# A decoder step on one core: the long output projections as a 2x2 block product in seven multiplications

## What is computed

```python
def conv_ffn(h, prev, w_in, conv_w, conv_b, w_out):
    a, v = jnp.split(h @ w_in, 2, axis=-1)              # 1024 -> 2 x 2816, "up"
    a, buf = causal_dwconv(a, prev, conv_w)             # 3 taps over the tokens
    return (jax.nn.silu(a + conv_b) * v) @ w_out, buf   # g (1032 x 2816) @ (2816 x 1024), "down"
...
    h = rmsnorm(x, norm_ffn_pre) * (1 + sc2) + sh2
    o, buf = conv_ffn(h, ...)
    x = x + g2 * rmsnorm(o, norm_ffn_post)
```

## Time and profile before

| | |
|---|---|
| median of 3 runs | 2589.6 us (2580.55 to 2592.13) |
| profiled execution: its own time, its span | 2581.3 us, 2579.5 us |
| TensorE busy, weight loads | 2450.6 us (95%), 2323.9 us (90%) |
| VectorE, ScalarE, GpSimd busy | 1628.6 us (63%), 947.8 us (37%), 139.7 us (5%) |
| mean granted TensorE clock | 0.981 |
| memory read, written | 289.2 MB, 51.8 MB |

### The profile page before, as it was taken

The page is one execution under the profiler, slowest core; times in us unless marked ns, Lnnn a source line. Parts: engine busy times, 40 slices in busy tenths (PEclk is TensorE's granted clock), DMA queues, the critical chain, the costliest instruction groups (busy, mean ns, idle before and its releaser), DMA issues. The chain is left out here.

```text
span 2579.5 us, 44995 instructions
## 1 busy us (share of the span) xinstructions
PE 2450.6 (95%) x19182; PEld 2323.9 (90%) x19182; DVE 1628.6 (63%) x2523; ACT 947.8 (37%) x1636; POOL 139.7 (5%) x213
## 2 busy tenths in 40 slices
PE   7999999989999999999999998789989999999997
PEld 5888999989999989999975887569989999989996
DVE  6422247887777765665455666967887777764553
ACT  4211124533333334543334664024533333334432
POOL 1000000000000010000002000210000000010000
PEclk8999999999999999999999999899999999999998
DMA  9677232222222265655010033872222222265653
GB/s 351 224 259 271 87 97 97 94 82 75 75 75 88 72 209 181 189 171 181 17 33 21 21 145 129 333 272 78 83 91 75 75 75 78 83 202 181 180 174 109
DMA packets 325191, 343.70 MB, mean 133 GB/s; under 512 B 14701, under 2 KB 297106, under 8 KB 312381
## 3 DMA queue, kind: packets, MB, share of 16 engines
q1 hardware_dynamic: 301393, 205.48, 26.0%
q0 software_dynamic: 23600, 135.35, 13.8%
HBM read 289.19 MB, written 51.82 MB: 132 GB/s over the span
## 5 line engine op out<-in xcount | busy, mean ns | idle before, releaser
L1587 DVE TENSOR_TENSOR w_lo<-w_raw,w_hi 128x1024 fp32r<-128x1024 f32 (+1 forms) x198 | 227.0, 1158 | 199.3 <-ACT w_hi L1056 195.3
L1056 ACT ACTIVATE w_hi<-w_raw 128x1024 fp32r<-128x1024 f32 (+1 forms) x198 | 197.2, 1006 | 303.6 <-DMA w_raw<-in_ffn_w_out 146.5
L2505 PE MATMUL ps<-h_hi,w_hi 128*128 128x344 f32 x816 | 265.5, 325 | 4.6 <-DVE latn L2153 3.8
L2507 PE MATMUL ps<-h_hi,w_lo 128*128 128x344 f32 x816 | 261.9, 321 | 0.0
L2506 PE MATMUL ps<-h_lo,w_hi 128*128 128x344 f32 x816 | 261.9, 321 | 0.0
L2565 PE MATMUL ps<-h_hi,w_hi 128*128 128x344 f32 x608 | 196.5, 323 | 3.4 <-DVE w_lo L1587 1.7
L2567 PE MATMUL ps<-h_hi,w_lo 128*128 128x344 f32 x608 | 194.2, 319 | 0.0
L2566 PE MATMUL ps<-h_lo,w_hi 128*128 128x344 f32 x608 | 194.0, 319 | 0.0
L1324 ACT ACTIVATE op_hi_Y<-op_raw_Y 128x512 fp32r<-128x512 f32 x80 | 50.5, 632 | 327.0 <-DVE op_raw_Y L2021 164.8
L2505 PEld LDWEIGHTS ps<-h_hi,w_hi 128*128 128x128 f32 x816 | 154.8, 190 | 9.3 <-issue 8.3
L2507 PEld LDWEIGHTS ps<-h_hi,w_lo 128*128 128x128 f32 x816 | 154.6, 189 | 0.0
(11 more groups left out here) (422 smaller groups left out, 6353.6 us busy)
## 6 DMA issues: line engine op xcount, KB each, us to landing
w_raw<-in_ffn_w_out SPq DMA_DIRECT2D x96, 512.0 KB, 4.1
...
w_raw<-in_ffn_w_out SPq DMA_DIRECT2D x48, 384.0 KB, 3.4
xc<-x_d POOLq DMA_DIRECT2D x12, 1376.0 KB, 7.2
x_d<-xc POOLq DMA_DIRECT2D x9, 1376.0 KB, 5.8
...
```

Source lines behind the costliest of these rows:

```text
L1056: act.activation(w_hi[k.slot][:, 0:k.kt, :], w_raw[k.slot][:, 0:k.kt, :], ACT.Copy).then_inc(hi_ready, 1)
L1587: dve.tensor_tensor(w_lo[k.slot][:, 0:k.kt, :], w_raw[k.slot][:, 0:k.kt, :], w_hi[k.slot][:, 0:k.kt, :].bitcast(F32), ALU.subtract).then_i ...
L2505: pe.matmul(o, w_hi[k.slot][:, t, :], h_hi[:, t, up_cols(c)], start=t == 0, stop=False)
L2507: ins = pe.matmul(o, w_lo[k.slot][:, t, :], h_hi[:, t, up_cols(c)], start=False, stop=t == KD - 1)
```

## The change

Two thirds of the tokens (c = 0 and 1) are now computed as a product of 2x2 blocks: the 22 K-tiles are two halves of 11, the 8 output tiles two halves of 4, and the thirds are the two token blocks. Seven products P1 to P7 of 4 tiles each replace eight. A product tile is 33 matmuls in two weight blocks of 6 and 5 K-tiles (`PARTS11`). The last third is computed as before, in blocks of 6, 6, 6 and 4. All blocks of the stage go through five slots of 6 K-tiles, so there are 56 + 32 = 88 blocks instead of 72.

- Four products (P6, P7, P5, P4) need sums of weight blocks. GpSimd's queue makes them in memory (`wsum_d`) during the up stage, by copying transfers and transfers that add to their destination (`weight_sums`), 44 per layer, one part after each of 16 stores of g; each part waits for the part before.
- Four products (P6, P7, P5, P3) need sums of activation blocks. VectorE makes them (`stage_sum`, four sums of 11x344 columns) in the place where h stood (`hh`), after GpSimd has loaded the blocks there; each operand then passes ScalarE and VectorE as pieces of 3 to 8 K-tiles (`piece_hi`, `piece_lo`, `HI_AT`, `LO_AT`).
- Results are put together from P1's copy and the banks (`combine`); products P2, P7, P3 and P4 add on in banks that an earlier product left.
- Two of the three thirds are finished after the product tiles: the scaling of third 0 stands in product tile 26, that of third 1 among the tiles of the last third, as `xk`, `od_sb` and `ss_d`.
- The tail transposes stand after the first product tile, in banks 3, 4, 6 and 7.

```diff
--- before.py
+++ after.py
-PARTS22 = [(0, 8), (8, 16), (16, 22)]
+PARTS22 = [(0, 6), (6, 12), (12, 18), (18, 22)]
+KW = KF // 2
+PARTS11 = [(0, 6), (6, KW)]
...
+WOPS = ["P1", "P2", "P6", "P7", "P5", "P3", "P4"]
+PIECES = {"P1": (0, 1), "P2": (2, None), "P6": (3, 4), "P7": (5, 6), "P5": (7, 8), "P3": (9, 10), "P4": (11, 12)}
+NPC = 17
+NW = len(WOPS) * KH * len(PARTS11)
...
+            loads[RAW_SEM[s]] += 16 * (dmas[n] if dmas else 1)
+            held = max([last[s]] + [last[u] for u in SHARED.get(s, ())])
...
-    after = [[4, 2, 3, 0, 1][n % 5] for n in range(NU * KD * len(PARTS22))]
-    down_kt = [k1 - k0 for k0, k1 in PARTS22] * (KD * NU)
+    down_kt = [k1 - k0 for k0, k1 in PARTS11] * (len(WOPS) * KH) + [k1 - k0 for k0, k1 in PARTS22] * KD
+    after = [9 + n % 5 for n in range(len(down_kt))]
...
+    d_at = [A_W + n * D6 for n in (6, 4, 8, 0, 2)]
...
+                            if t == 2 * KH:
+                                sp.wait_ge(wsum_in, 16 * 44 * (l + 1))
...
+            def weight_sums(l, f):
+
+                q, part = f // 4, f % 4
+                rows = slice(q * ROWS, (q + 1) * ROWS)
+                low = slice(KW * P + q * ROWS, KW * P + (q + 1) * ROWS)
+                c1, c2 = slice(0, KH * P), slice(KH * P, KD * P)
+                w, v = ffn_w_out[l], wsum_d[l]
+                if part:
+                    pool.wait_ge(wsum_in, 16 * (44 * l + 11 * q + (4, 8, 10)[part - 1]))
+                if part == 0:
+                    pool.dma_start(v[0][rows, :], w[rows, c1]).then_inc(wsum_in, 16)
...
+                elif part == 1:
+                    pool.dma_start(v[0][rows, :], w[rows, c2], accum_op=ALU.add).then_inc(wsum_in, 16)
...
+                elif part == 2:
+                    pool.dma_start(v[1][rows, :], w[low, c2], accum_op=ALU.add).then_inc(wsum_in, 16)
...
+                    pool.dma_start(v[3][rows, :], w[low, c1], accum_op=ALU.add).then_inc(wsum_in, 16)
...
+            LO_AT = {5: (3,), 6: (4,), 9: (5,), 10: (6,), 13: (7,), 14: (8,), 17: (9,), 18: (10,), 21: (11,), 22: (12,),
+                     23: (13,), 25: (14,), 26: (15,)}
+            SUM_AT = {2: (0,), 3: (1,), 4: (2,), 11: (3,)}
+            ADD_AT = {5 + s: s for s in range(KH)}
+            ADD_AT.update({13 + s: s for s in range(KH, 15)})
...
+                    if stage != "sc" and 2 <= f < 18:
+                        weight_sums(int(stage == "f1"), f - 2)
...
+            def wino_moves(d):
+
+                ready = AL0[DOWN[d]]
+                pool.wait_ge(al_ready, ready + 7)
+                load_stage(1, stage_r[0], act_d[1, :, KW:KF, :])
+                pool.wait_ge(al_ready, ready + 9)
+                load_stage(2, stage_r[1][:, 0:3, :], act_d[2, :, KF - 3:KF, :])
+                pool.wait_ge(al_ready, ready + 11)
+                load_stage(0, h_raw[:, :, up_cols(2)], act_d[2, :, KW:KW + KD, :])
+                pool.wait_ge(w_done, wino_block(d, 6 * KH - 1, 1).done)
+                load_piece(d, 14, act_d[2, :, 0:7, :])
+                load_piece(d, 15, act_d[2, :, 7:KW, :])
+                pool.wait_ge(w_done, wino_block(d, 7 * KH - 1, 1).done)
+                load_x(d, 1)
...
+                for t in range(len(WOPS) * KH):
+                    i0, op, j = b + 2 * t, WOPS[t // KH], t % KH
+                    hi_to(i0 + 4)
+                    if op == "P1":
+                        copy_one(d, j)
+                    if op == "P2":
+                        copy_two(d, j)
+                    hi_to(i0 + 5)
+                    if op in ("P5", "P3", "P4"):
+                        square_tile(d, KH * (("P5", "P3", "P4").index(op) + 1) + j)
+                    for i in HI_AT.get(t, ()):
+                        piece_hi(d, i)
+                    if t == 25:
+                        root(q_post(d, 0))
...
+                out, x, y, op = ((a22, a21, a22, ALU.subtract), (a21, a11, a21, ALU.subtract), (a11, a22, a11, ALU.subtract),
+                                 (a12, a12, a11, ALU.add))[n]
...
+            def combine(d, t):
+
+                op, j = WOPS[t // KH], t % KH
+                l = d // 2
+                one, up = od_sb[:, j, :], KH + j
+                o = bank((BANKS_B if op in ("P6", "P7", "P4") else BANKS_A)[j])[:, 0:UC]
+                dve.wait_ge(w_done, wino_block(d, t, 1).done)
+                if op in ("P6", "P7"):
+                    dve.wait_ge(one_copied, KH * l + j + 1)
+                    out, x, y, f = (o_sb if op == "P6" else od_sb)[:, up, :], one, o, ALU.add
+                elif op == "P4":
+                    out, x, y, f = one, one, o, ALU.add
+                else:
+                    out = (od_sb if op == "P5" else o_sb)[:, up, :]
+                    dve.wait_ge(comb_done, 20 * l + (KH if op == "P5" else 0) + j + 1)
+                    x, y, f = o, out, ALU.subtract
+                dve.tensor_tensor(out, x, y, f).then_inc(comb_done, 1)
...
+                for t in range(len(WOPS) * KH):
+                    i0, op = b + 2 * t, WOPS[t // KH]
+                    lo_to(i0 + 4)
+                    if op not in ("P1", "P2"):
+                        combine(d, t)
+                    if t in ADD_AT:
+                        add_wino(d, ADD_AT[t])
+                    lo_to(i0 + 5)
+                    if t == 0:
+                        tails_out(KF, t0)
+                    for n in SUM_AT.get(t, ()):
+                        stage_sum(d, n)
+                    for i in LO_AT.get(t, ()):
+                        piece_lo(d, i)
+                    if t == 25:
+                        inv_root(q_post(d, 0))
+                    if t == 26:
+                        rs_in(q_post(d, 0))
+                        scale_tiles(d, 0, G, range(KD))
...
+                    if more and m == 2:
+                        rs_in(q_post(d, 1))
+                        scale_tiles(d, 1, G, range(KD))
...
+                if op == "P2":
+                    pe.wait_ge(one_copied, KH * l + j + 1)
+                if op == "P6" and j == 0:
+                    pe.wait_ge(tail_e, 2 + 6 * (l + 1))
+                if op in ("P7", "P3", "P4"):
+                    pe.wait_ge(comb_done, 20 * l + {"P7": 0, "P4": KH, "P3": 2 * KH}[op] + j + 1)
+                if op == "P5":
+                    pe.wait_ge(o_e, 24 * d + j + 1)
...
+                        hi, lo = operand(o, k)
+                        pe.matmul(out, w_hi[w.slot][:, k - k0, :], hi, start=op in ("P1", "P6", "P5") and k == 0, stop=False,
+                                  skip_group_check=True)
+                        pe.matmul(out, w_hi[w.slot][:, k - k0, :], lo, start=False, stop=False, skip_group_check=True)
+                        ins = pe.matmul(out, w_lo[w.slot][:, k - k0, :], hi, start=False, stop=k == KW - 1,
+                                        skip_group_check=True)
+                        if k in between:
+                            between[k]()
+                    ins.then_inc(w_done, 1)
...
+            def down_long(d, nt, t0):
+
+                more, j0 = d < 3, NU * (d + 1)
+                q0, q1 = q_post(d, 0), q_post(d, 1)
+                for t in range(len(WOPS) * KH):
+                    between = {26: {0: lambda: stat_o(q0, d, 0)}, 27: {0: lambda: spread_o(q0, d, 0)}}.get(t, {})
+                    wino_tile(d, t, between)
+                    if t == 0:
+                        tails(KF, nt, t0)
+                yt = 0
...
```

More of the change, by code:

```diff
@@ L73, in block_plan @@
 def block_plan():
-    last, loads = [0] * 9, [0] * 9
+    last, loads = [0] * 14, [0] * 9
     blocks, first = [], {}
@@ L237, in build @@
     assert off + 3 * U4 <= A_W
+    od_sb = at("od_sb", [P, KD, UC], A_U + 2 * KD * U4)
+    off = A_U + 3 * KD * U4
+    sqd = [at(f"sqd{i}", [P, UC], off + i * U4) for i in range(2)]
+    ss_d = [at(f"ss_d{i}", [P, UC], off + (2 + i) * U4) for i in range(2)]
+    assert off + 4 * U4 <= A_W
     c0 = [A_C]
@@ new lines, in third_out @@
+            def third_out(d, m, between):
+                l = d // 2
+                if m < 3:
+                    pe.wait_ge(comb_done, 20 * l + (19, 20, 13)[m])
+                else:
+                    pe.wait_ge(o_e, 24 * d + o_before(d, 2, m) + 1)
+                o = bank(o_tile(d, 2, m))[:, 0:UC]
+                ready = {0: 15, KW - 4: 16, KW: 14, KW + KD: 17}
+                for n, (k0, k1) in enumerate(PARTS22):
+                    w = down_block(d, 2, m, n)
+                    pe.wait_ge(w_ready, w.done)
+                    for k in range(k0, k1):
+                        if m == 0 and k in ready:
+                            pe.wait_ge(al_ready, AL0[DOWN[d]] + ready[k])
+                        hi, lo = third_tile(k)
+                        pe.matmul(o, w_hi[w.slot][:, k - k0, :], hi, start=k == 0, stop=False)
+                        pe.matmul(o, w_hi[w.slot][:, k - k0, :], lo, start=False, stop=False)
+                        ins = pe.matmul(o, w_lo[w.slot][:, k - k0, :], hi, start=False, stop=k == KF - 1)
```

(5 more changed lines are left out.)

632 lines of the change are left out of this document (391 added, 241 removed).

## The result

The changed kernel takes 2599.55 us in the median of 20 runs (2592.98 to 2606.68), the kernel before 2586.13 in as many (2580.55 to 2592.13). The ratio is 1.005, 95% interval 1.0041 to 1.0058: slower by 13 us. I had said 2567 and faster. The profiled execution has a span of 2598.3 us where that of before has 2579.5, 18.8 more.

What follows compares the result with a forecast made beforehand. TensorE was taken to bound the kernel, with VectorE and ScalarE keeping ahead. The terms, -41.5 + 7.8 + 2 + 5.4 + 3.3 + 5 + 0 = -18.0 on a base of 2585.5, gave 2567 us, range 2545 to 2602.

Steps and rivals of the forecast that it cites:

- Term 1: Long output projections: 264 fewer TensorE matmuls in both layers at 0.157 us each, 41.5 us off.
- Term 2: Transition from up to down product: TensorE idles 3.5 us for the gate, 5.6 for tail copies; +7.8, bounds 0 and +16.
- term 3: First eight product tiles: VectorE's blocks, sums and pieces fit with 1 to 3 us to spare; +2, bounds 0 and +12.
- Term 4: Normalisation beside the weights: VectorE's scaling and additions delay weight blocks; +5.4 in layer 0, +3.3 in layer 1, bounds 0 and +20.
- Term 5: Clock: TensorE at half speed for 4 to 6 us after pauses at the transition and in normalisation; +5, bounds 0 and 12.
- Term 6: Weight sums on GpSimd's queue in the up stage: 88 transfers of 704 KB, 5 us each, cost 0.
- rival D: Up stage: adding transfers from 8.8 us each, one by one, hold up g's stores and TensorE; near 2880, chance 0.07.
- C: Product stages: weight blocks land late in every round of five slots; 2609 at 1.2 us over the window, chance 0.12.
- B: Product stages: VectorE and ScalarE pace the product, VectorE over 88% busy; 2584, no change, chance 0.20.
- A: Product stages: the order costs nothing more than before, with added costs near 4 us; 2548, chance 0.13.

Runs made afterwards that it cites:

- Experiment 2: Changed kernel with the three stage loads of 1.7 to 1.9 MB issued behind the last store of g: 2592.36 us, ratio 1.0013.
- experiment 1: Changed kernel with the up product's last gate ahead of the third and fourth weight block on ScalarE and VectorE: 2596.43 us, ratio 1.0036.
- Experiment 4: Changed kernel with layer 0's second-third scaling split around a weight block, and the next stage's second block split before the last third's scaling: 2592.25 us, ratio 1.0014.
- experiment 11: Changed kernel with 115 extra matmuls of 128 columns per layer, result unread, ahead of the tail transposes: 2597.6 us, ratio 1.0054.
- Experiment 10: Changed kernel with 200 extra matmuls of 128 columns per layer, result unread, ahead of the tail transposes: 2605.32 us, ratio 1.0064.
- experiment 8: Changed kernel with plain copies for the seven adding transfers of each group, so the result is wrong: 2599.73 us, ratio 1.0057.
- experiment 12: Changed kernel with serial stage loads, tails behind the second tile, normalisation reordered, activation sums halved and moved earlier, tail copies ahead of blocks: 2565.34 us, ratio 0.9926.

## Why the prediction was wrong

**Term 1** was right: the count and 0.157 us.

**Term 2 is the step that failed.** It gave +7.8 for both layers and bounds of 0 and +16; measured +25.2, outside them. The order of the queues was followed well: the wait for the gate, then the one for the copies, in those two places. The second was 3.85 where 5.6 was said; the first was 13.27 where 3.5 was said. What was wrong is the wait for the weight block "in front" of the gate. Term 2 gives it no time at all and has the gate done at 938.3, which holds only if the block lands there as fast as the 3.5 us that term 3 takes from the earlier trace rows. Measured, the block landed 18.4 us after its issue and the gate was done at 950.3. The upper bound named the mechanism, the stage loads of 1.7 to 1.9 MB, but looked for late *pieces*. The pieces came nearly in time; the blocks behind them did not. Of rows 7 the number to take was the 12.0 at the far end, a block of 512 KB beside two loads of 1376 KB; here up to four transfers of 1.2 to 1.9 MB were in flight. Experiment 2 shows it (loads moved, landings back to 8 and 5 us, 13.27 becomes 4.77, no engine's order changed), experiment 1 that the order alone doesn't decide.

**Term 3** gave +2, measured +5.5, within its bounds of 0 and 12. The walk of the first tiles came out nearly as written (waits of 0.2 to 1.2 us).

**Term 4** was right in place and size: 5.4 and 3.3 said, 6.2 and 3.4 measured, and the row of 5 us stands in layer 0's fourth last-third tile, released by a weight's low half. Experiment 4 took it away.

**A term is missing.** The next stage's weight slots share memory with the product's five slots: its second block could only be issued at 1206.6, landed 4.0 us later, reached VectorE's queue behind the scaling of 7.3 us, and cost +4.1. Experiment 4 removed 3.1 of it together with most of term 4's row. I had followed the diff's slots inside the product and not to the stage behind it.

**Term 5** gave +5 and an upper bound of 12, measured +12.7. Of this 6.5 are matmuls at half speed (112 starts 0.2 to 0.36 us apart, against 56 before), 3.3 the transposes of the tails (3.58 us for 16 at half speed, 1.91 in experiment 11), and the other 2.9 I put down to the first matmuls behind each wait, whose rows are 0.40 to 0.66 us long; that part is not measured by itself. The number is of busy time. What the time itself lost to the clock at the transition is less: experiment 11 cut the half speed in layer 0's transition from 20.5 us to 3.4, its layer 0 is 1.2 us shorter from the end of the up product to the wait before `oa_lo_Xb`, and its ratio is no lower than the changed kernel's (1.0054 against 1.005). The Trainium skill (TensorE: Matmul & The Clock Gate, Part 1: The HAM clock gate) has it that activity releases the clock. Experiment 10 agrees: with TensorE kept busy, no stretch at half speed stands around either pause. That alone doesn't tell whether anything waits for the work in such a stretch.

**Term 6** was right at 0. The stores of g stay 20.28 us apart (starts 878.29 and 898.57), TensorE is as busy in the window of the earlier trace rows as before, with the DMA engines at 64% instead of 26%, and experiment 8 found no difference. The window:

```profile
500.00:900.00 400.00, 391.50 (x3200) 390.82 (x3198) 310.22 (x434) 132.38 (x199) 52.62 (x64) 0.99 0.64 158
```

The 5 us a transfer taken for it was wrong (10.8), and it did no harm: 11 x 10.8 = 119 us of transfers in a group of 81 us is more than one by one would allow, but only its four parts wait for each other, not each transfer. So rival D's price of 8.8 us a transfer was passed without its harm: its condition, one by one, was not the kernel's.

**The rivals.** C, late weight blocks on the slower side, was the nearest, with 0.12: 2609 against 2599.55. Its mechanism was right, its place was not: it had the lateness spread over all 88 blocks, at 9.6 us throughout, where it is 10 to 20 us over five blocks a layer, and it argued against itself with the median landing. B (VectorE and ScalarE pace the product) is out: VectorE is 69% and 64% busy in the two stages, below B's sign of 88%, and it had 6.06 us idle at the place where most was lost, waiting for a block itself. A came true in no run: its time was 2548, and experiment 12, the fastest, has 2565. That lies at the forecast of 2567, but this is a repaired schedule with other waits and doesn't bear the forecast's sum out.

What stays open is how the queues share the DMA engines. The landings give the effect for these sizes and this order; no run here varied the size of one packet or the number of queues.
